# Shifting the projections against the attention steps of a decoder trunk kernel: three products ahead, forms exchanged later

## What is computed

```python
h = rms_norm(x, norm_g[l])
proj = jnp.einsum('bsd,de->bse', h, w_in[l])
u_pool, z_pool, q, k, v, z_attn, gate_logits = jnp.split(proj, splits, axis=-1)
y_pool = multiscale_pool(u_pool, pool_w[l], pool_scale[l]) * jax.nn.silu(z_pool)
attn = stick_breaking_attention(q, k, v)          # 8 heads of 64, strictly causal
y_attn = attn * jax.nn.silu(z_attn)
gates = jax.nn.sigmoid(gate_logits + b_gate[l]).reshape(B, S, 2, D)
merged = (gates[:, :, 0] * jnp.einsum('bsp,pd->bsd', y_pool, w_pool_up[l])
          + gates[:, :, 1] * jnp.einsum('bsa,ad->bsd', y_attn, w_attn_up[l]))
x = x + jnp.einsum('bsd,de->bse', merged, w_out[l])
return rms_norm(x, final_g)
```

## Time and profile before

| | |
|---|---|
| median of 3 runs | 1575.68 us (1573.25 to 1582.23) |
| the profiled execution | 1579.27 us |
| its span | 1577.4 us |
| block front | to about 372.7 us |
| stage3 | about 372.7 to 1244 us |
| TensorE matmul busy | 1530.4 us, 97% |
| VectorE, GpSimd, ScalarE busy | 1237.2, 1102.0, 856.2 us |

### The profile page before, as it was taken

The page is one execution under the profiler, slowest core; times in us unless marked ns, Lnnn a source line. Parts: engine busy times, 40 slices in busy tenths (PEclk is TensorE's granted clock), DMA queues, the critical chain, the costliest instruction groups (busy, mean ns, idle before and its releaser), DMA issues. The chain is left out here.

```text
span 1577.4 us, 24982 instructions
## 1 busy us (share of the span) xinstructions
PE 1530.4 (97%) x7770; PEld 1275.2 (81%) x7770; DVE 1237.2 (78%) x1592; ACT 856.2 (54%) x1653; POOL 1102.0 (70%) x770
## 2 busy tenths in 40 slices
PE   7999999998999999999998999999999999999998
PEld 5787878886888887888877888888888788888886
DVE  7968595766987788887897887798878656687987
ACT  6546554444666665666665676666766512233342
POOL 4899876985977678777766776787756334456774
PEclk9999999999999999999999999999999999999999
DMA  7468942465344343343694442443423688764552
GB/s 270 151 240 310 376 125 92 118 214 169 87 109 112 89 127 102 94 139 93 185 329 143 129 120 87 120 114 99 121 71 83 209 272 257 251 197 166 181 190 110
DMA packets 170803, 254.45 MB, mean 161 GB/s; under 512 B 48417, under 2 KB 82209, under 8 KB 170674
## 3 DMA queue, kind: packets, MB, share of 16 engines
q1 hardware_dynamic: 170674, 252.85, 51.2%
HBM read 166.80 MB, written 85.99 MB: 160 GB/s over the span
## 5 line engine op out<-in xcount | busy, mean ns | idle before, releaser
L2103 POOL TENSOR_TENSOR ring<-raw,ring 128x512 fp32r<-128x512 f32 x140 | 241.2, 1723 | 154.3 <-ACT ring L1950 143.9
L2045 DVE TENSOR_TENSOR_SCAN left<-keep,left 128x512 f32<-128x512 f32 x192 | 283.8, 1478 | 61.9 <-issue 40.1
L1870 PE MATMUL psum<-hT,ring 128*128 128x512 f32 x664 | 273.9, 412 | 14.7 <-ACT sum_a L1983 5.1
L1874 PE MATMUL psum<-hT,ring 128*128 128x512 f32 x664 | 271.8, 409 | 0.0
L1872 PE MATMUL psum<-hT,ring 128*128 128x512 f32 x664 | 271.2, 408 | 0.0
L1956 ACT ACTIVATE keep<-psum 128x512 f32<-128x512 f32 (+3 forms) x320 | 170.8, 534 | 131.8 <-PE psum L1893 119.2
L1963 ACT ACTIVATE wt<-psum 128x512 fp32r<-128x512 f32 (+3 forms) x320 | 171.0, 534 | 111.3 <-PE psum L1901 108.6
L2051 DVE TENSOR_TENSOR wt<-psum,wt 128x512 fp32r<-128x512 f32 (+3 forms) x320 | 190.3, 595 | 16.5 <-ACT wt L1963 13.9
L1913 PEld LDWEIGHTS psum<-wt,vm 128*128 128x128 f32 x1088 | 171.6, 189 | 26.9 <-DVE wt L2051 1.5
L1913 PE MATMUL psum<-wt,vm 128*128 128x256 f32 x1088 | 181.5, 281 | 1.0 <-DVE wt L2051 1.0
L1901 PE MATMUL psum<-ident,left 128*128 128x128 f32 x1088 | 171.1, 272 | 4.0 <-DVE wt L2051 4.0
(11 more groups left out here) (262 smaller groups left out, 3410.1 us busy)
## 6 DMA issues: line engine op xcount, KB each, us to landing
raw<-in_w_strips SPq DMA_DIRECT2D x144, 256.0 KB, 4.0
qm<-qk_scratch SPq DMA_DIRECT2D x128, 128.0 KB, 4.5
gate<-gate_scratch SPq DMA_DIRECT2D x64, 256.0 KB, 4.7
form_scratch<-hT SPq DMA_DIRECT2D x28, 512.0 KB, 7.0
hT<-form_scratch SPq DMA_DIRECT2D x28, 512.0 KB, 8.3
km<-qk_scratch SPq DMA_DIRECT2D x64, 128.0 KB, 3.7
merged_scratch<-rows SPq DMA_DIRECT2D x32, 256.0 KB, 5.0
mt<-merged_scratch SPq DMA_DIRECT2D x16, 512.0 KB, 5.8
```

The source lines that it names most:

```text
L1870: pe.matmul(o, hi, m_hi, start=k == 0 and not onto, stop=False, skip_group_check=onto)
L1874: last = pe.matmul(o, lo, m_hi, start=False, stop=k == HK - 1, skip_group_check=onto)
L2045: dve.tensor_tensor_scan(left[:, n % LN, span][:, ::-1], k, k, carry, ALU.mult, ALU.bypass).then_inc(scanned, 1)
L2103: pool.tensor_tensor(out_, a, b, op).then_inc(s, 1)
```

## The change

`READY_PARTS` goes from 2 to 3. The third product, (0, S2), adds onto the bank of the first, (0, A11), so ScalarE must first copy that one out: this `take` moves from stage3 into front, into a tile that both share.

```diff
-READY_PARTS = 2
+READY_PARTS = 3
...
+                if g == FRONT_GROUPS:
+                    act.wait_ge(mixed, 2 * MIXED_FIRST)
+                act.activation(ready_sum if g == FRONT_GROUPS else sum_u if j == S2 else sum_a, bank(g, j), ACT.Copy
+                               ).then_inc(taken, 1)
...
-                if r is not None and r < FRONT_PARTS:
+                if r is not None and r <= FRONT_PARTS:
                     g, j = divmod(r, FORMS)
                     if j in FRONT_TAKE:
                         take(g, j)
```

The results of the last group of each half (groups 5 and 11) are finished one slot after their product and not two:

```diff
-        at_slot = [r for r, last in zip(lagged, (False, True))
-                   if r is not None and r < FRONT_PARTS and (r == FRONT_PARTS - 1) == last]
+        at_slot = [r for r, soon in zip(lagged, (False, True))
+                   if r is not None and r < FRONT_PARTS and (r // FORMS % HALF_GROUPS == HALF_GROUPS - 1) == soon]
```

The table of stage3 gives the first 160 steps less filler and moves the calm stretch back by 17 steps:

```diff
-    calm = range(ALL // 2 - 14, ALL // 2 + 18)
-    cost = [x * (0.8 if s in calm else 1.0) for s, x in enumerate(cost)]
+    LATER = 17
+    calm = range(ALL // 2 + LATER - 14, ALL // 2 + LATER + 18)
+    cost = [x * (0.89 if s < ALL // 2 else 1.0) * (0.8 if s in calm else 1.0) for s, x in enumerate(cost)]
```

ScalarE finishes a result with `k % 4 == 3` ahead of the step's sigmoid, and in step 0 copies weights ahead of it; VectorE does its silu ahead of the scan:

```diff
+                for k in at(RESULT, s):
+                    if k % 4 == 3:
+                        result(k)
+                if s == 0:
+                    for w in at(W_STEP, s):
+                        split_w(w)
                 if 0 <= s < ALL:
                     remaining(s)
-                for w in at(W_STEP, s):
-                    split_w(w)
+                if s > 0:
+                    for w in at(W_STEP, s):
+                        split_w(w)
...
                 for k in at(RESULT, s):
-                    result(k)
+                    if k % 4 < 3:
+                        result(k)
...
+                for k in at(RESULT, s):
+                    if kind(k // 4) < 2 and k % 4 == 3:
+                        silu(k)
                 if s - AV_LAG - 1 in LAST:
                     add_halves(s - AV_LAG - 1)
                 if s < ALL:
                     scan(s)
```

More of the change, by code:

```diff
@@ L275, in build @@
         head_loads = HeadLoads(sem, heads, qk_d, v_d)
+        ready_sum = heads("sum_a", [P, CH])[:, :]
         front(nc, sem, psum, at, free_at, hT_at, ident, ident_r, gcol, bcol, pscol, v_ends, hT, ring, raws, staging, ring_at, raw1_at,
-              x, x_T, norm_gT, w_v, b_gateT, pool_scaleT, w_strips, pool_w, pool_fix, v_d, qk_d, mix_d, form_d, head_loads)
+              x, x_T, norm_gT, w_v, b_gateT, pool_scaleT, w_strips, pool_w, pool_fix, v_d, qk_d, mix_d, form_d, head_loads, ready_sum)
         w_at = free_at - 5 * KT * P * 4
@@ L318, in front @@
 def front(nc, sem, psum, at, free_at, hT_at, ident, ident_r, gcol, bcol, pscol, v_ends, hT, ring, raws, staging, ring_at, raw1_at,
[L319 removed]
+          x, x_T, norm_gT, w_v, b_gateT, pool_scaleT, w_strips, pool_w, pool_fix, v_d, qk_d, mix_d, form_d, head_loads, ready_sum):
     G = len(WINDOWS)
@@ L1026, in take @@
                     act.wait_ge(summed, 3 * (g - 1) + FRONT_ADD[S3 if j == A11 else S4])
-                act.activation(sum_u if j == S2 else sum_a, bank(g, j), ACT.Copy).then_inc(taken, 1)
+                if g == FRONT_GROUPS:
+                    act.wait_ge(mixed, 2 * MIXED_FIRST)
+                act.activation(ready_sum if g == FRONT_GROUPS else sum_u if j == S2 else sum_a, bank(g, j), ACT.Copy
+                               ).then_inc(taken, 1)
             def close_u(g):
@@ L1494, in stage3 @@
 def stage3(nc, sem, psum, sb, raws, ring, ident, bcol, v_ends, hT, w_strips, mix_t, mix_d, yp_d, za_d,
-           at_d, gate_d, form_d, form_in, staging, sum_stored, y_stored, opening, head_loads):
+           at_d, gate_d, form_d, form_in, staging, sum_stored, y_stored, opening, head_loads, sum_a):
     ITEMS = attention_items()
@@ L1654, in stage3 @@
     RESULT = [fin[result_part(k)] + 1 for k in range(RESULTS)]
+    assert all(a < b for a, b in zip(RESULT, RESULT[1:]))
     FORM_STEP = {}
@@ L1673, in stage3 @@
     blocks = [{**raws[i], S1: raws[i][A11], S4: raws[i][A12], S2: second} for i in range(2)]
-    sum_a, sum_b, sum_c, sum_d = (sb(f"sum_{n}", [P, CH])[:, :] for n in "abcd")
+    sum_b, sum_c, sum_d = (sb(f"sum_{n}", [P, CH])[:, :] for n in "bcd")
     res, sum_e = staging[:, 0, :], staging[:, 1, :]
@@ L2003, in _ @@
             act.sem_inc(w_hi_done, RING)
+            act.sem_inc(taken, 1)
             for s in range(-9, END):
@@ L2008, in _ @@
                     for j in TAKE:
-                        if s == PART_END[part(g, j)]:
+                        if s == PART_END[part(g, j)] and part(g, j) > 0:
                             take(g, j)
+                for k in at(RESULT, s):
[4 more added lines that the diff above has]
+                        split_w(w)
                 if 0 <= s < ALL:
                     remaining(s)
-                for w in at(W_STEP, s):
-                    split_w(w)
+                if s > 0:
+                    for w in at(W_STEP, s):
+                        split_w(w)
                 if 0 <= s - T_LAG < ALL:
@@ L2087, in _ @@
                 for k in at(RESULT, s):
-                    if kind(k // 4) < 2:
+                    if kind(k // 4) < 2 and k % 4 < 3:
                         silu(k)
```

3 lines of the change are left out of this document (1 added, 2 removed).

## The result

The changed kernel takes 1587.84 us, median of 6 runs (1585.30 to 1589.87); the kernel before took 1575.6 us beside it (1573.25 to 1582.23). The ratio is 1.0063, 95% interval 1.0046 to 1.0079. That is 12.2 us more by the medians, where the prediction had 0.7 less. The whole interval lies above 1, and the ratio is above the 0.5% that the prediction took as the bound of no change.

A forecast was written before the change was run, and what follows sets the result against it. TensorE bounds the kernel, matmuls filling 97% of the span, so only its idle and low-clock stretches could change. Terms -1.8 - 2.2 - 4.5 + 1.0 + 6.8 = -0.7 gave 1575.0 us from the median, range 1563 to 1585.

The forecast's parts named there:

- Term 1: Between the halves of front, results one slot earlier remove TensorE's wait for tile `b`: -1.8 us, bounds 0 to -1.9.
- Term 2: At the barrier, a third product ahead cuts idle time from 5.07 to 2.9 us, ending on `sum_b`: -2.2 us.
- Term 3: A22 results ahead of sigmoid and scan remove six waits for `sum_d`: -4.5 us, bounds -5.4 to -2.
- Term 4: Less filler in the first 160 steps cuts VectorE's slack; waits for `wt` may grow: +1.0 us, bounds 0 to +3.
- Term 5: Mid-kernel exchange of forms: later loads raise its cost from 9.5 to 16.3 us: +6.8, bounds about 0 and +17.
- the 4.15 us nearly vanish: Between the halves, the copy of `b` on ScalarE would hardly wait for its store, which goes 3.9 us sooner.
- form 6: In the exchange, three loads behind a `load_mix` awaiting result 49 make it late by 10 us, bounds 6.7 and 16.
- Form 5: In the exchange, its loads land in the shadow of form 4's stall of about 2.5 us, adding no cost.
- The clock: In the exchange, one fall of the granted clock, after the long form stall, costing 2.6 us.
- the third rival: GpSimd's backlog holds SP at the exchange: it costs 24.4 us, +14.9 against before; total 1583.1 to 1585.6. Chance 0.17.
- E + 5.3: In the exchange, when TensorE needs form 6: 5.3 us after E, the end of product (12, 4).
- The case of the clock that stays up: At the barrier, 2.9 us idle leaves the clock up: alone -3.3 us, 1572.4 us. Chance 0.25.

The follow-up runs named there:

- x2: The kernel before with only the results of groups 5 and 11 in front one slot earlier: ratio 1.0023.
- x7: The changed kernel with group 5's results two slots behind their product again, as in the kernel before: ratio 1.0038.
- x3: The kernel before with only three products ahead, the `take` in front and the early weight copies of step 0: ratio 0.9997.
- x4: The kernel before with only the A22 results ahead of sigmoid and scan: 1569.45 us, ratio 0.9932.
- x1: The kernel before with only the new table of filler (LATER = 17, factor 0.89): ratio 1.0107.
- x5: The changed kernel with `load_mix(51)` and the store of result 49 moved behind the last form load in SP's order: ratio 0.9983.
- x6: The changed kernel with two form loads per step in place of one: 1570.72 us, ratio 0.9940.
- x11: The kernel before with only the factor 0.89 on the first 160 steps, the calm stretch where it was: ratio 1.0090.
- x9: The changed kernel with forms 3 to 6 loaded two per step and group 5's results as before the change: 1564.97 us, ratio 0.9913.
- x10: The change without the table and without group 5's earlier results, against the kernel before: 1570.49 us, ratio 0.9953.
- x12: x10 with forms 4 to 6 loaded two per step: 1566.65 us, ratio 0.9927 to the kernel before.
- x8: The kernel before with A22 results first, as in x4, and two form loads per step: ratio 0.9999.

## Why the prediction was wrong

By its own terms, in us; the runs are of one part alone, by their ratios:

| term | forecast | by the traces | by runs |
|---|---|---|---|
| 1 results of the halves | -1.8 | wait for `b` -1.9; new wait +3.9 and clock +1.7 | x2 +3.6, x7 +3.9 |
| 2 three products ahead | -2.2 | idle -2.2, clock about -1 | x3 -0.5 (-3 to +2) |
| 3 A22 results first | -4.5 | waits -5.4 | x4 -10.7 |
| 4 less filler | +1.0 | `wt` -1.1; `sum_c`, `staging` +2.7 | in x1, without `sum_c` and `staging` |
| 5 the exchange | +6.8 | 24.1 against 9.5: +14.6 | x1 +16.9 with term 4 |
| behind stage3 | none | +5.2 | no tie to a part seen |

**Term 1 had the wrong sign.** The store did go earlier and `b` lost its wait, as said. The step that failed is "the 4.15 us nearly vanish", which followed only the store that was moved forward. It left out what is queued behind the moved instructions: on ScalarE the copy of (5, A12) now stands ahead of a `take`, and its tile is not free until a store has landed that took 7.6 us. The bounds (0 to -1.9) left out a loss for no stated reason. This is 5.5 us of the miss, and x2 and x7 show it.

**Term 5 was too small by half, and its mechanism was right for form 6 only.** SP stood at `load_mix(51)` for result 49, the last three loads went out behind it, and form 6 was late by 10.1 us, as said to 0.1. x5, which moves that one wait, takes 12.6 us off (by the trace some 9), against 10 + 2.6 in the sum. What failed stands in three places. *Form 5* was to land in the shadow of form 4: it cost 3.1 us of its own. The prediction held form 4's last load behind the store of result 48, until 8 us behind the product; SP in fact stood 6.5 us at the weight load ahead of it, and six loads of forms 4 and 5 followed one after another from 818.77 to 827.36 us. The stall for form 4 came out near (3.1 us for 2.5), by another way than the one given. *The clock* fell three times in the middle and not once: behind q 1.7 us, behind form 5 1.7 and behind form 6 1.8 (5.8 or 5.9 us of busy time at 0.71, 0.71 and 0.69), where the sum had one of 2.6. Behind form 4 it stayed at 1.00. *q* was put at 1.2 us and cost 2.6. Against the forecast's 16.3 us for the exchange the traces have 18.9 us of waits and 5.2 of clock, 24.1.

That form 6 came out right hides two errors that cancel. `times_mix` of result 49 did not end 7.5 us behind its product but 11.0: (12, 4) ended at 833.0, and POOL at 844.05. This is over the 9 us from which the third rival was to decide, and that rival's total is near: it had 24.4 us for the exchange, +14.9 against before, and the trace has 24.1 and +14.6. **But it is near by luck.** Result 48 was not late: its `times_mix` ended 5.9 us behind its product, not 9.8. Form 4 cost 3.1 us and not 5, with no fall of the clock; form 6 cost 10.1 and not 13; the rest is form 5, q and falls that the rival did not have.

Nor was result 49 late for GpSimd's backlog: POOL stood idle 4.73 us before 840.01. TensorE had itself just stopped for form 5, 3.08 us, and the steps of attention that GpSimd's work waits for stopped with it. A late load delays the result that SP waits for, and that delays the next loads. The other traces bear this out. From the end of (12, 4) to the end of result 49's `times_mix` it is 7.1 us in x6, with no wait for form 5; 7.7 in x5 (0.8 us of wait), 8.0 in x7 (1.1), 8.8 in x11 (2.0), 11.0 in the changed kernel (3.1) and 13.4 in x1 (4.4). Of the kernels with less filler ahead of step 160 only x9 does not fit, with 11.2 us and no such wait; there POOL stood 3.42 us for a load of v. So the 7.5 us of the prediction was about right for a queue without stalls. The trace of before had the other case: its own result 49 took 12.9 us, from 830.24 to 843.10, behind a form wait of 3.9 us, and the prediction took result 50's 7.5.

On the other side the need came later too, and for the same reason: at 843.1 us and not at E + 5.3, which with E = 833.0 is 838.3; the wait for form 5 and the clock behind it are the 4.8 us between. x7 shows nearly the case of the prediction: `times_mix` at E + 8.0, the last load there at E + 17.0, the need at E + 6.5, and form 6 late by 10.7 us. So the stall is of this size with either error or with neither.

The loads themselves took what the rows had said: from 844.57, when the first of the last three went out, to 853.18 are 8.6 us, where the prediction's steps make 8.9 (from E + 7.95 to E + 16.8; it writes 8.3). The estimate of 6.4 us from the Trainium skill, DMA: Bandwidth & Descriptors, Bandwidth and Anatomy of one DMA, is too short here, by 2.2 us. The 2 us in it are given there for transfers that GpSimd issues, and these are issued by SyncE.

**Term 3 was right in the waits, and too small alone.** All six are gone, and terms 3 and 4 together (forecast -3.5) show as 4.0 us less idle time in the 400 us before the exchange. Behind it nothing was gained: a wait for `sum_c` (1.5 us, at 929) and one for `staging` (1.5 us, at 1039) stand where x4 has no idle time at all (358.00 us busy of 358). Neither x4 nor x1 has a wait of that size for them. All five kernels with the new table, the A22 results first and three products ahead have both. Term 3's own run gave 10.7 us because the clock also stayed up in the middle. **Term 4's** fear, that waits for `wt` grow, did not come: they shrank.

**Term 2 was right,** idle time and releaser included. The case of the clock that stays up did not come in the changed kernel. It came in x10 and x12, see below.

**Behind stage3** the profiled execution is 5.2 us longer, with no term for it. x7, with all but one small part of the change, does not have it, and x8, with the old table, and x1, with the new one, have most of it; one profiled execution each speaks against a tie to the change, and does not settle the cause. The profile of after was the slowest of its six runs, and what single executions show there of `y_lo` should not be put on the change.

Put together by the traces: term 1 missed by 5.5 us, term 5 by 7.8 and the block behind stage3 by 5.2, while terms 2 to 4 and small waits of front gave some 4 us more than forecast. That is 14 or 15 us, where the spans have a miss of 11.3; the falls of the clock are read from windows and sum to more than the 2.2 us by which the busy time grew, so this much doesn't close. The range did not hold the result because the bounds of term 1 had no upper side, and because the bad cases of term 5 (form 5 late, more falls of the clock, q late) were held to be one rival of 0.17, when in the traces they come together, from the same loads standing too late.

## What to carry to other kernels

When needs and loads are both moved by a table, count the margin of each load in steps before and after first: here 4, 2, 1 became 2, 0, -2. Then look in the queue for what stands ahead of each load and waits for another engine: here a weight load and a `load_mix`, and moving the latter away took most of the 10 us stall off at the same margin. But loads pulled 13 steps ahead pushed the next transfers late and gave it all back. When an instruction is moved forward on an in-order engine, look at what frees its own operand and at who is queued behind it; "earlier" cost 3.6 us here because the tile's last store had not landed. Parts that are good alone (A22 first: -10.7 us) can be hidden by one that is bad, so time the parts singly: the table and the results of the halves lost here, and with their faults mended the same change gives 0.9913 in place of 1.0063. The new table itself was not needed for that: x12 has the old one and 0.9927.

## What the runs showed of the hardware

The clock behind an idle stretch of the same length is not the same each time. At the barrier, with 3.0 us idle and the same matmuls behind it, the granted clock stayed at 1.00 in x10 (2.97 us idle) and x12 (2.96), and fell in x9 (3.01) and in the changed kernel (2.86, to 0.56). The window of x10, and then of x9:

```profile
373.84:377.00 3.16, 3.16 (x14) 2.63 (x15) 0.00 (x0) 0.42 (x1) 2.87 (x3) 1.00 0.51 124
```

```profile
374.14:377.00 2.86, 2.86 (x7) 2.30 (x8) 0.00 (x0) 0.42 (x1) 2.57 (x3) 0.55 0.54 138
```

Shorter stops had falls too: behind 2.25 us for q, x9's clock was 0.63 and then 0.77, and behind 1.83 us for q, x10's was 0.52. The longer stop of 3.07 us for form 4 in the changed kernel had none, at 1.00, nor had that of 3.28 us in x1:

```profile
827.50:830.50 3.00, 2.93 (x15) 2.52 (x16) 0.56 (x1) 1.25 (x3) 0.05 (x1) 1.00 0.95 286
```

So a length of idle time between 1.8 and 3.3 us does not say whether the clock falls. Nor is a fall that stays away at one stop a gain that is kept: in x10 and x12 the clock fell at the next stop instead, 2.52 us for `wt` some 12 us later, where x9 and the changed kernel, with 2.2 us there, stayed at 1.00. In x10 the 3 us behind it:

```profile
388.40:391.40 3.00, 3.00 (x14) 2.62 (x15) 3.00 (x3) 0.80 (x2) 2.69 (x3) 0.66 0.01 2
```

What a fall costs varied as well: 2.6 us before at the barrier, 1.7 to 1.8 us at five places of the changed kernel. A forecast should carry it as a chance at each stop, here about 1.7 us. And form loads of 512 KB took somewhat longer to land where more of them stood together: from 770 to 812 us a median of 8.7 us in x4 (17 loads, 5.8 to 12.4), and of 9.8 us in x8 (20 loads, two per step, 6.4 to 15.5).
